# Token halves around the post-norms of the second block, and a weight ring with the low parts written over the raw weights

## The chip, the cores and the metric

One Trainium2 chip, one NeuronCore. The metric is the device time of one launch in microseconds (us). Short names as in the profile: PE is TensorE, DVE VectorE, ACT ScalarE, POOL GpSimd, SP SyncE, which issues the weight DMAs.

## The reference

Two transformer blocks run one after the other on 256 tokens (rows) of width 2048, all in fp32. What matters here is the second block, two layers deep:

```python
for layer in range(DEPTH_2):                          # 2
    h = rms_norm_2(x, mix_pre_g[layer])
    m = mixer_ab(h, ...) if layer % 2 == 0 else mixer_cd(h, ...)   # ends in concat(...) @ w_out
    x = x + rms_norm_2(m, mix_post_g[layer])          # post-norm
    h = rms_norm_2(x, ffn_pre_g[layer])
    f = channel_mixer(h, ...)                         # up, causal conv, gelu(gate) * val, down
    x = x + rms_norm_2(f, ffn_post_g[layer])          # post-norm
```

So there are four post-norms. Each needs the whole row of `m` or `f` (all 2048 columns) before one column of the new `x` is known, and the next projection needs the new `x`, transposed. Three of them are followed by a projection and are called seams here (after `mixer_ab`, after the first `channel_mixer`, after `mixer_cd`); the fourth ends the kernel.

## The kernel before

All weights are read once, as chunks of 256 contraction rows by 512 columns (`CHUNK`, 512 KB; some are narrower), about 1,140 of them. fp32 accuracy is had by splitting every operand in a high and a low part in fp32r: ACT copies a raw chunk to `w_hi` (`split_hi`, L271), DVE subtracts to get `w_lo` (`split_lo`, L277), and PE multiplies each of the two k-tiles of a chunk three times (hi·hi, hi·lo, lo·hi, L302 to L304) for each token half `tt` of 128 rows: 12 matmuls of 512 columns a chunk, in `mm_chunk`. Eight chunks make a block of 512 output columns, accumulated in two PSUM banks (`acc`), one for each token half.

The order of all work is written by hand, engine by engine, with counting semaphores. SP loads chunk after chunk into `raw`, a ring of 8 slots, and issues the load of chunk k when `lo_done` says that chunk k-8 has been split. `w_hi` and `w_lo` are rings of 4 slots (`SPLIT`), so `split_hi` of chunk k also waits until PE has used chunk k-4 (`chunk_used`). DVE and ACT have the splits some four chunks ahead of PE in their programs, with the work on results between them.

```python
wait(sp, lo_done, 8 * q + k - RING + 1)            # load_chunk
wait(act, raw_in[k % RING], 16 * (q + k // RING + 1))   # split_hi
wait(act, chunk_used, 8 * q + k - SPLIT + 1)
```

At a seam the last output block (b = 3) has four chunks in a mixer and eight in an ffn. PE finishes all chunks of it for both token halves, DVE adds the PSUM result to what was kept before (`macc`, L1898 or L1849), ACT squares it (`squares`, L1216, with the sum per row), DVE sums (L1565, L1566), ACT takes the root (L1221, with the load of its function table), DVE the reciprocal (L1570), and `normed` (L1859) adds the scaled row to `xres` for both halves of a 512-column slice. Meanwhile POOL multiplies each slice of `macc` by the gain of the post-norm (`scaled_out`, L850), and `normed` waits for that (`merged`). Then `turn` (L341) transposes a slice of `xres` in 8 matmuls, `turn_hi` (L350) and `turn_lo` (L366) write it as `l_hi` and `l_lo`, and the first projection block runs its chunks with the next `turn` after chunks 1, 3 and 5 (`new_x`, and `turns` in `mm_block`). The gain of the pre-norm goes in with the transposes; the pre-norm's own 1/rms multiplies the projection's output later.

Other places where PE waits for a chain of ACT and DVE are the pooling and index work of `mixer_ab` (L1048, L1063) and the recurrent and attention inputs of `mixer_cd` (L1167, L341, `turned_in`). In both, weights that PE reads straight from `raw` (two chunks each) take slots of the ring; before, they too are split, for nothing. Early in the kernel, POOL loads bias rows for the attention (L814) while narrow chunks (width 268, `A_TAIL`) pass through PE.

Of the kernel before, what the change touches and what calls it, by code (L numbers as in the profile page):

```python
# [16 lines left out]
F32 = mybir.dt.float32  # L17
# [101 lines left out]
def build_program(nc, d):  # L119

    with ExitStack() as ctx:
# [54 lines left out]
        stat_v, stat_a = sem("stat_v"), sem("stat_a")  # L176
        at_t, at_qk, at_s, at_l, at_mx, at_e, at_r, at_p = [sem("at_" + n) for n in ("t", "qk", "s", "l", "mx", "e", "r", "p")]
        at_pt, at_ptc, at_pv, at_pvg, at_ohi, at_o = [sem("at_" + n) for n in ("pt", "ptc", "pv", "pvg", "ohi", "o")]
        out_st, out_ready = sem("out_st"), sem("out_ready")
# [86 lines left out]
        def split_hi(act, q, ks, n=CHUNK):  # L266

            for k in ks:
                wait(act, raw_in[k % RING], 16 * (q + k // RING + 1))
                wait(act, chunk_used, 8 * q + k - SPLIT + 1)  # L270
                nc.scalar.activation(w_hi[:, k % SPLIT, 0:n], raw[:, k % RING, 0:n], ACT.Copy).then_inc(hi_done, 1)  # L271

        def split_lo(dve, q, ks, n=CHUNK):

            for k in ks:
                dve.wait_ge(hi_done, 8 * q + k + 1)
                nc.vector.tensor_tensor(w_lo[:, k % SPLIT, 0:n], raw[:, k % RING, 0:n], w_hi[:, k % SPLIT, 0:n].bitcast(F32),  # L277
                                        ALU.subtract).then_inc(lo_done, 1)

        def a_width(k):  # L280
            b, c = A_ORDER[k] if k < len(A_ORDER) else (0, 0)
            return CHUNK if b is None else 2 * A_BLOCKS[b][1]

        def split_hi_a(act, k0, k1):
            for k in range(k0, k1):
                split_hi(act, 0, (k,), a_width(k))

        def split_lo_a(dve, k0, k1):
            for k in range(k0, k1):
                split_lo(dve, 0, (k,), a_width(k))  # L290

        def mm_chunk(pe, q, k, lhs, kts, out, first, last, w=BW):

            pe.wait_ge(lo_done, 8 * q + k + 1)
            hi = w_hi[:, k % SPLIT, 0:len(kts) * w].rearrange("p (a b) -> p a b", b=w)
            lo = w_lo[:, k % SPLIT, 0:len(kts) * w].rearrange("p (a b) -> p a b", b=w)
# [8 lines left out]
            m.then_inc(chunk_used, 1)  # L305

# [285 lines left out]
        gpost_mix = late[:, 0:D]  # L592

# [35 lines left out]
        T_X1, T_PU, T_ABX, T_F0, T_FX, T_CD, T_CQ, T_QR, T_CDX, T_F1 = 29, 33, 35, 39, 55, 59, 63, 65, 67, 71  # L629
# [15 lines left out]
        HALVES = [t + b for t in (0, T_O, T_X1, T_ABX, T_FX) for b in range(4)] + [T_CQ] + [T_CDX + b for b in range(4)]  # L645
        X_ROWS = {T_ABX: 16, T_FX: 20, T_CDX: 24}
# [21 lines left out]
        A_ORDER += [(5, c) for c in range(NCH)]  # L668
        A_END = [A_ORDER.index((b, NCH - 1)) + 1 for b in range(6)]
# [25 lines left out]
        def _(sp):  # L695
# [85 lines left out]
            for b in range(4):  # L781
                sp.wait_ge(out_ready, b + 1)
                sp.dma_start(d["out"][:, BW * b:BW * (b + 1)].rearrange("(t p) n -> p t n", p=P),
                             xres[:, :, BW * b:BW * (b + 1)]).then_inc(out_st, 16)
# [3 lines left out]
        def _(pool):  # L788
# [54 lines left out]
            def scaled_out(squares0, gwide, gains_in):  # L843

                pool.wait_ge(*gains_in)
                for b in range(4):
# [42 lines left out]
        def _(pe):  # L889
# [11 lines left out]
            def cmp_chunk(n, k):  # L901
# [5 lines left out]
                whi = w_hi[:, k % SPLIT, :].rearrange("p (a b) -> p a b", a=4)  # L907
                wlo = w_lo[:, k % SPLIT, :].rearrange("p (a b) -> p a b", a=4)
# [206 lines left out]
            def mixer_out(q, o, u, other, us, n, e, g):  # L1115
# [8 lines left out]
                out_chunks(q, o, u, OUT_ENDS[0] - 4, OUT_ENDS[3])  # L1124

            def new_x(x_t):

                return lambda b: turn(pe, x_t + b, xres[:, :, BW * b:BW * (b + 1)], (rows_ready, X_ROWS[x_t] + b + 1))

            def ffn(q, o, u, t, x_t, h):  # L1130

                for g in range(2):
                    def pair(j, first=False):
# [3 lines left out]
                        def mine():  # L1137
                            turn(pe, t + 8 * g + 2 * j, hid2, (acc_free, u + 12 * g + 2 * j + 1))
                        mm_block(pe, q + 12 * g + 2 * j, u + 12 * g + 2 * j, 0 if u % 2 == 0 else 1, lh, k0=o,
                                 need=(lhs_ready, x_t) if first and g == 0 else None, hook=None if first else before,  # L1140
                                 turns=new_x(x_t) if first and g == 0 else None)
# [4 lines left out]
                    for b in range(4):  # L1146
                        def last():
                            turn(pe, t + 8 * g + 7, hid2, (acc_free, u + 12 * g + 8))
                        mm_block(pe, q + 12 * g + 8 + b, u + 12 * g + 8 + b, (u + b) % 2, mh, k0=o,
                                 need=(hid_ready, h + 4 * g) if b == 0 else None, hook=last if b == 0 else None)  # L1150

            mixer_out(Q_ABO, O2, U_ABO, (pool_dve, 6), ud, N_D, E_D, G_D)
            ffn(Q_F0, O2, U_F0, T_F0, T_ABX, 0)
# [18 lines left out]
            for b, (c, w) in enumerate(CD_BLOCKS):  # L1172
# [33 lines left out]
            ffn(Q_F1, O6, U_F1, T_F1, T_CDX, 8)  # L1206

        @block.scalar
        def _(act):
            aseq = [0]  # L1210

            def squares(rows, col, sums):
                for tt in range(2):
# [3 lines left out]
                                             accum_out=sums[:, tt, col:col + 1]).then_inc(squares_done, 1)  # L1217

# [186 lines left out]
            def mixer_out(q, o, u, us, n, e, g, k, t, gain):  # L1405
# [3 lines left out]
                for b, end in enumerate(OUT_ENDS):  # L1409
                    split_hi(act, q, range(o + at, o + end + SPLIT))  # L1410
                    at = end + SPLIT
                    act.wait_ge(acc_free, u + 3 + b + 1)
                    squares(macc[:, :, BW * b:BW * (b + 1)], b, ssp)
                new_x(q + 4, o, k, t, gain)

            def new_x(q, o, k, t, gain):

                root(k, ST["root"], ST["mean"])
                for b in range(4):
                    turn_hi(act, t + b, tiles(lh, 4 * b), gain[:, 4 * b:4 * b + 4])  # L1420
                    squares(xres[:, :, BW * b:BW * (b + 1)], b, ssp)
                    if 0 < b < 3:
                        split_hi(act, q, (o + 2 * b + 2, o + 2 * b + 3))
# [687 lines left out]
```

## Time and profile before

| | us |
|---|---|
| runs, median (lowest to highest) | 3404.14 (3403.9 to 3407.31), 3 runs |
| the profiled execution | 3407.14 |
| its span, first to last instruction | 3405.4 |
| PE busy / DVE busy / ACT busy | 3291.9 / 1948.1 / 1664.9 |
| PE not busy in the span | 113.5 |

Mean granted TensorE clock in the span: 0.987. The profiled execution is 1.7 us longer than its span, and 3.0 us above the median of the runs. PE is the engine to watch: an idle microsecond there is a microsecond of the kernel, and idle time of the others counts only where PE waits for it.

### The profile page before, as it was taken

How to read it: one execution, taken by the hardware profiler on the slowest of the kernel's cores; microseconds unless marked ns; L12 is line 12 of the kernel's file. 1: busy time of each engine (PE TensorE's matmuls, PEld its weight loads, DVE VectorE, ACT ScalarE, POOL GpSimd, SP SyncE). 2: the span in 40 equal slices, each digit the busy share in tenths (PEclk: the TensorE clock that was granted, in tenths of full speed). 3: DMA queues.
4: the chain of work that ended last, by engine and by line, in shares of the span. 5: the costliest groups of instructions: out<-in, count | busy, mean ns of one | idle time of the engine just before them, and what ended most of it. 6: DMA issues, size and time to landing. Idle time of an engine off the chain costs nothing.

```text
span 3405.4 us, 41414 instructions
## 1 busy us (share of the span) xinstructions
PE 3291.9 (97%) x15346; PEld 2737.7 (80%) x15346; DVE 1948.1 (57%) x2331; ACT 1664.9 (49%) x2256; POOL 184.7 (5%) x199
## 2 busy tenths in 40 slices
PE   8999999999999999999999899999989798999998
PEld 7888778888888888888877788888878677888886
DVE  5566545555555555556555666556655656664665
ACT  5555544444444444445444455445545645553553
POOL 0023100000000000001001100000000011000001
PEclk9999999999999999999999999999989899999999
DMA  8845556666666666655565556566554544656653
GB/s 258 235 140 154 165 177 193 189 185 193 187 190 191 188 184 190 192 175 172 153 192 159 183 162 185 190 187 184 185 159 127 169 138 161 184 188 195 184 180 131
DMA packets 324437, 608.82 MB, mean 179 GB/s; under 512 B 19468, under 2 KB 46424, under 8 KB 323632
## 3 DMA queue, kind: packets, MB, share of 16 engines
q1 hardware_dynamic: 320768, 594.05, 56.7%
q0 software_dynamic: 3504, 12.52, 1.3%
q8 instruction: 109, 1.79, 0.2%
q14 instruction: 56, 0.46, 0.0%
HBM read 603.22 MB, written 3.28 MB: 178 GB/s over the span
## 4 chain that ended last, share of the span: by engine, by line
PE 94%; DVE 2%; ACT 1%; issue 1%; DMA 0%; POOL 0%; SPq 0%; DVEq 0%; ACTq 0%
PE ps L302 29%; PE ps L304 29%; PE ps L303 29%; PE ps L341 2%; PE ps L444 1%; PE ps L468 1%; ACT w_hi L271 1%; DVE w_lo L277 0%; PE ps L433 0%; POOL main L834 0%; PE ps L470 0%; DVE xres L1859 0%; DVE stats L1566 0%; PE ps L446 0%; PE ps L914 0%
## 5 line engine op out<-in xcount | busy, mean ns | idle before, releaser
L277 DVE TENSOR_TENSOR w_lo<-raw,w_hi 128x1024 fp32r<-128x1024 f32 (+1 forms) x1142 | 1420.7, 1252 | 1244.3 <-ACT w_hi L271 1239.3
L271 ACT ACTIVATE w_hi<-raw 128x1024 fp32r<-128x1024 f32 (+1 forms) x1142 | 1197.0, 1054 | 1509.3 <-PE ps L304 1472.8
L302 PE MATMUL ps<-w_hi,l_hi 128*128 128x512 f32 (+2 forms) x2848 | 1113.4, 391 | 14.0 <-issue 6.4
L303 PE MATMUL ps<-w_lo,l_hi 128*128 128x512 f32 (+2 forms) x2848 | 1098.9, 386 | 1.5 <-issue 1.5
L304 PE MATMUL ps<-w_hi,l_lo 128*128 128x512 f32 (+2 forms) x2848 | 1099.3, 386 | 0.0
L302 PEld LDWEIGHTS ps<-w_hi,l_hi 128*128 128x128 f32 x2848 | 538.0, 189 | 121.7 <-issue 10.8
L302 PE MATMUL ps<-w_hi,m_hi 128*128 128x512 f32 (+1 forms) x1600 | 624.0, 390 | 10.4 <-DVE main L1883 5.5
L304 PEld LDWEIGHTS ps<-w_hi,l_lo 128*128 128x128 f32 x2848 | 537.7, 189 | 107.0
L303 PEld LDWEIGHTS ps<-w_lo,l_hi 128*128 128x128 f32 x2848 | 538.5, 189 | 102.1 <-issue 1.9
L304 PE MATMUL ps<-w_hi,m_lo 128*128 128x512 f32 (+1 forms) x1600 | 620.0, 387 | 0.0
L303 PE MATMUL ps<-w_lo,m_hi 128*128 128x512 f32 (+1 forms) x1600 | 619.9, 387 | 0.0
L302 PEld LDWEIGHTS ps<-w_hi,m_hi 128*128 128x128 f32 x1600 | 302.2, 189 | 71.4 <-DVE main L1883 6.2
L304 PEld LDWEIGHTS ps<-w_hi,m_lo 128*128 128x128 f32 x1600 | 302.1, 189 | 61.3
L303 PEld LDWEIGHTS ps<-w_lo,m_hi 128*128 128x128 f32 x1600 | 302.3, 189 | 59.5
L1914 DVE SCALAR_TENSOR_TENSOR main<-ps,main 128x255 f32<-128x255 f32 (+1 forms) x256 | 105.8, 475 | 19.9 <-ACT main L1449 18.8
L1227 ACT ACTIVATE main<-ps,stats 128x512 f32<-128x512 f32 (+2 forms) x170 | 104.9, 667 | 9.5 <-PE ps L304 9.4
L341 PE MATMUL ps<-ident_sb,main 128*128 128x128 f32 x494 | 65.6, 276 | 13.9 <-DVE main L2035 4.3
L850 POOL TENSOR_TENSOR main<-main 128x1024 f32<-128x1024 f32 x8 | 19.1, 2386 | 1088.0 <-ACT ps L1216 1088.0
L341 PEld LDWEIGHTS ps<-ident_sb,main 128*128 128x128 f32 x494 | 57.9, 142 | 23.7 <-DVE main L2035 4.7
L341 PE MATMUL ps<-ident_sb,xres 128*128 128x128 f32 x192 | 30.0, 308 | 41.3 <-DVE xres L1859 27.9
L366 DVE SCALAR_TENSOR_TENSOR l_lo<-ps,pk_sb,l_hi 128x256 fp32r<-128x256 f32 x96 | 39.8, 476 | 47.3 <-ACT l_hi L350 47.3
L350 ACT ACTIVATE l_hi<-ps,pk_sb 128x256 fp32r<-128x256 f32 x96 | 37.6, 473 | 55.7 <-PE ps L341 55.6
(293 smaller groups left out, 1544.0 us busy)
## 6 DMA issues: line engine op xcount, KB each, us to landing
raw<-ffn_up SPq DMA_DIRECT2D x256, 512.0 KB, 4.1
raw<-w_in SPq DMA_DIRECT2D x176, 512.0 KB, 3.7
raw<-w_mlp_in SPq DMA_DIRECT2D x128, 512.0 KB, 3.8
raw<-w_mlp_out SPq DMA_DIRECT2D x128, 512.0 KB, 3.9
raw<-ffn_down SPq DMA_DIRECT2D x128, 512.0 KB, 4.6
raw<-ab_w_in SPq DMA_DIRECT2D x64, 512.0 KB, 3.8
raw<-w_branch SPq DMA_DIRECT2D x48, 512.0 KB, 3.9
raw<-cd_w_in SPq DMA_DIRECT2D x40, 512.0 KB, 4.3
```

The costliest lines, as they stand in the source:

```text
L271: nc.scalar.activation(w_hi[:, k % SPLIT, 0:n], raw[:, k % RING, 0:n], ACT.Copy).then_inc(hi_done, 1)
L277: nc.vector.tensor_tensor(w_lo[:, k % SPLIT, 0:n], raw[:, k % RING, 0:n], w_hi[:, k % SPLIT, 0:n].bitcast(F32), ALU.subtract).then_inc(lo_ ...
L302: nc.tensor.matmul(o, xh, hi[:, j, :], start=first and j == 0, stop=False)
L303: nc.tensor.matmul(o, xh, lo[:, j, :], start=False, stop=False)
L304: m = nc.tensor.matmul(o, xl, hi[:, j, :], start=False, stop=last and j == len(kts) - 1)
L341: m = nc.tensor.transpose(tp4[:, j, tt * P:(tt + 1) * P], rows[:, tt, j * P:(j + 1) * P], ident[:])
L350: i = nc.scalar.activation(dst[0][:, j, :], tp4[:, j, :], ACT.Copy, scale=gain[:, j:j + 1])
L366: i = nc.vector.scalar_tensor_tensor(dst[1][:, j, :], tp4[:, j, :], gain[:, j:j + 1], dst[0][:, j, :].bitcast(F32), ALU.mult, ALU.subtract)
L444: m = nc.tensor.matmul(o, qs[:, tt * P:(tt + 1) * P], kt[:, 0:w], start=True, stop=u.rope is None)
L468: m = nc.tensor.matmul(o, u.v[0][0:kk, :], pts[0:kk, 0:TOK], start=u.first, stop=u.last and len(u.v) == 1)
L1227: i = nc.scalar.activation(dst(tt), acc(par, w)[:, tt, :], func, scale=scale[:, tt:tt + 1])
L1914: i = nc.vector.scalar_tensor_tensor(dst[:, x, n:], tp4[:, x, 0:TOK - n], fcw[:, 2 - n, k:k + 1], dst[:, x, n:], ALU.mult, ALU.add)
```

## The change

Three parts.

1. **The seams by token halves.** The last four chunks before a post-norm are multiplied first for token half 0 (`last_chunks`, first loop), then for half 1. While PE does half 1, DVE, ACT and DVE carry half 0 through the add (`last_half`), the square and root (`post_root`), the reciprocal and `normed`, now on 128 rows by 512 columns each. PE's turns are of 4 transposes (`turn_half`), each into PSUM banks of its own pair (`x_bank`, banks 4 to 7 in turn). The next block's first four chunks are again multiplied by halves (`first_block`). The gain product of slice 3 goes from POOL to DVE. The function table for the root is loaded early (`sqrt_table`). The squares are written to SBUF (`junk`) instead of PSUM. The fourth post-norm, at the end, goes by halves as well, and the output is stored by halves.
2. **The ring.** `w_lo` lies over `raw` (8 slots, written in place), and `w_hi` has 8 slots. So `split_hi` waits for its load alone, and the load of chunk k waits until PE has used chunk k-8.
3. **Widths.** Chunks that are narrower than 512 columns are split at their own width throughout (`WIDTH`: the three `AB_TAIL` blocks of 368 columns, the last of `mixer_cd`'s, of 320), and the four chunks that PE reads raw are not split at all.

The diff below is cut to the ring, PE's two new functions, the first half of ACT's `seam`, and SP's stores at the end.

```diff
-        raw = sb("raw", [P, RING, CHUNK])
-        w_hi = sb("w_hi", [P, SPLIT, CHUNK], F32R)
-        w_lo = sb("w_lo", [P, SPLIT, CHUNK], F32R)
+        raw_guard = nc.sbuf_tensor("raw", [P, RING, CHUNK], F32)
+        raw = raw_guard.__enter__()
+        raw_guard.__exit__(None, None, None)
+        w_lo = sb("w_lo", [P, RING, CHUNK], F32R)
+        w_hi = sb("w_hi", [P, RING, CHUNK], F32R)
...
-            wait(sp, lo_done, 8 * q + k - RING + 1)
+            wait(sp, chunk_used, 8 * q + k - RING + 1)
...
-                wait(act, chunk_used, 8 * q + k - SPLIT + 1)
...
+            def last_chunks(s, q, k, kt0, out, first):
+                for i in range(4):
+                    kt = kt0 + 2 * i
+                    m = mm_half(pe, q, k + i, mh, (kt, kt + 1), out, 0, first and i == 0, i == 3)
+                m.then_inc(tt_done, 1)
+                for i in range(4):
+                    kt = kt0 + 2 * i
+                    m = mm_half(pe, q, k + i, mh, (kt, kt + 1), out, 1, first and i == 0, i == 3)
+                    m.then_inc(chunk_used, 1)
+                    if s < 3 and i > 1:
+                        turn_half(s, i - 2)
+            def first_block(s, q, k, out):
+                def turned(c, tt):
+                    pe.wait_ge(xt_lo, 16 * s + 2 * X_TURNS.index((c // 2, tt)) + c % 2 + 1)
+                for c in range(4):
+                    turned(c, 0)
+                    mm_half(pe, q, k + c, lh, (2 * c, 2 * c + 1), out, 0, c == 0, False)
+                    if c > 1:
+                        turn_half(s, c)
+                for c in range(4):
+                    turned(c, 1)
+                    m = mm_half(pe, q, k + c, lh, (2 * c, 2 * c + 1), out, 1, c == 0, False)
+                    m.then_inc(chunk_used, 1)
+                    turn_half(s, 4 + c)
+                for c in range(4, NCH):
+                    turned(c, 1)
+                    mm_chunk(pe, q, k + c, lh, (2 * c, 2 * c + 1), out, False, c == NCH - 1)
...
+            def seam(s, q, o, k0, gain):
+                sqrt_table()
+                split_hi(act, q, range(o + k0, o + 4))
+                post_root(s, 0)
+                x_square(s, 0)
+                x_square(s, 1)
+                x_hi(s, 0, gain)
+                x_hi(s, 1, gain)
+                post_root(s, 1)
+                split_hi(act, q, (o + 4, o + 5))
...
+            for tt in range(2):
+                for h in range(2):
+                    sp.wait_ge(x_rows, 24 + 4 * tt + 2 * h + 2)
+                    sp.dma_start(d["out"][P * tt:P * (tt + 1), 2 * BW * h:2 * BW * (h + 1)],
+                                 xres[:, tt, 2 * BW * h:2 * BW * (h + 1)]).then_inc(out_st, 16)
```

DVE's part of a seam is `split_lo` of the chunks up to o+3, the sums of slices 0 to 2, `last_half` of half 0, `post_rstd`, `normed` of slices 0 and 1, `x_lo` of turn 0, then `last_half` of half 1, and so on. What each engine's program holds there:

ACT, at the first seam (after `mixer_ab`), before. The first two rows are the splits of the next projection's chunks 2 and 3; L1216 squares slice 3 of `macc`.

```order
L271 ACTIVATE w_hi<-raw 128x1024 [waits chunk_used,raw_in4]
L271 ACTIVATE w_hi<-raw 128x1024 [waits chunk_used,raw_in5]
L1216 ACTIVATE ps,stats<-main 128x512 [waits squares_done,acc_free]
L1216 ACTIVATE ps,stats<-main 128x512 [waits squares_done]
L1221 ACT_TABLE_LOAD
L1221 ACTIVATE stats<-stats 128x2 [waits stat_v]
L350 ACTIVATE l_hi<-ps,pk_sb 128x256 [waits tp_done]
L350 ACTIVATE l_hi<-ps,pk_sb 128x256 x3
```

The same place now. The first two rows square slice 2, whose result comes at the start of the last four chunks.

```order
L1320 ACTIVATE late,stats<-main 128x512 [waits squares_done,acc_free]
L1320 ACTIVATE late,stats<-main 128x512 [waits squares_done]
L1534 ACT_TABLE_LOAD
L1534 ACTIVATE stats<-ident_sb 128x1
L284 ACTIVATE w_hi<-raw 128x1024 [waits raw_in3]
L284 ACTIVATE w_hi<-raw 128x1024 [waits raw_in4]
L284 ACTIVATE w_hi<-raw 128x1024 [waits raw_in5]
L1320 ACTIVATE late,stats<-main 128x512 [waits squares_done,half_out]
L1530 ACTIVATE stats<-stats 128x1 [waits squares_done,post_v]
L1320 ACTIVATE late,stats<-xres 128x512 [waits squares_done,x_rows] x2
L1546 ACTIVATE l_hi<-ps,pk_sb 128x128 [waits xt_pe]
```

The splits wait for their load alone, and three of them and the table load now stand between the squares of slice 2 and the square of half 0 of slice 3.

DVE, at the same seam, before:

```order
L277 TENSOR_TENSOR w_lo<-raw,w_hi 128x1024 [waits hi_done] x4
L1898 TENSOR_TENSOR main<-ps,main 128x2x512 [waits acc_free,chunk_used]
L1565 TENSOR_REDUCE stats<-stats 128x2 [waits squares_done]
L1566 TENSOR_SCALAR stats<-stats 128x2 [waits dve_seq]
L1570 RECIPROCAL stats<-stats 128x2 [waits stat_a]
L1859 SCALAR_TENSOR_TENSOR xres<-main,stats,xres 128x512 [waits merged,stat_v]
```

and now:

```order
L2115 TENSOR_TENSOR main<-ps,main 128x2x512 [waits acc_free,chunk_used]
L295 TENSOR_TENSOR w_lo<-raw,w_hi 128x1024 [waits hi_done] x3
L2012 TENSOR_REDUCE stats<-stats 128x2 [waits squares_done]
L2013 TENSOR_SCALAR stats<-stats 128x2 [waits dve_seq]
L2023 TENSOR_TENSOR main<-ps,main 128x512 [waits gain_in,acc_free,tt_done]
L2026 TENSOR_TENSOR main<-main,late 128x512 [waits half_out]
L2034 RECIPROCAL stats<-stats 128x1 [waits post_a,dve_seq]
L2042 SCALAR_TENSOR_TENSOR xres<-main,stats,xres 128x512 [waits merged,dve_seq]
```

The add of slice 3 has become two, of which the first waits for half 0 alone (`tt_done`), behind three splits; the gain product (L2026) is new on DVE.

## Rows read from the trace of the kernel before

**Rows 1.** The page, busy time and share of the span

```profile
PE 3291.9 (97%) x15346; PEld 2737.7 (80%) x15346; DVE 1948.1 (57%) x2331; ACT 1664.9 (49%) x2256; POOL 184.7 (5%) x199
```

**Rows 2.** Who PE waited for: total us, times, longest

```profile
PE ps L341 <- DVE xres L1859: 27.9, 3, 9.3
PE ps L1063 <- issue: 6.7, 1, 6.7
...
PE ps L302 <- DVE m_lo L366: 4.4, 1, 4.4
...
PE ps L341 <- ACT main L1227: 3.7, 1, 3.7
```

**Rows 3.** Timeline of the first seam: start, us, engine, what, idle before

```profile
1947.57 0.39 PE L304 MATMUL ps<-w_hi,m_lo 128*128 128x512 f32 x1
1948.05 1.06 ACT L271 ACTIVATE w_hi<-raw 128x1024 fp32r<-128x1024 f32 x1 [1.66 <-PE ps L304]
1950.28 1.22 DVE L1898 TENSOR_TENSOR main<-ps,main 128x1024 f32<-128x1024 f32 x1
...
1955.78 2.74 DVE L1859 SCALAR_TENSOR_TENSOR xres<-main,stats,xres 128x512 f32<-128x512 f32 x4
1957.25 1.97 PE L341 MATMUL ps<-ident_sb,xres 128*128 128x128 f32 x8 [9.29 <-DVE xres L1859]
1961.10 0.77 PE L302 MATMUL ps<-w_hi,l_hi 128*128 128x512 f32 x1 [1.89 <-issue]
1966.30 1.04 PE L341 MATMUL ps<-ident_sb,xres 128*128 128x128 f32 x8
1972.66 1.04 PE L341 MATMUL ps<-ident_sb,xres 128*128 128x128 f32 x8
```

**Rows 4.** Window there: us, busy of PE PEld DVE ACT POOL, clock, DMA, GB/s

```profile
1961.10:1966.30 5.20, 5.20 (x13) 3.99 (x13) 2.00 (x4) 0.94 (x4) 0.00 (x0) 0.51 0.00 0
```

**Rows 5.** Groups by shape: count, busy us, mean ns of one

```profile
L350 ACT ACTIVATE l_hi<-ps,pk_sb 128x256 fp32r<-128x256 f32 x96 | 37.6, 473 | 55.7 <-PE ps L341 55.6
L1216 ACT ACTIVATE ps<-main 128x512 f32<-128x512 f32 x34 | 20.1, 592 | 47.4 <-DVE main L1849 28.0 <-DVE main L1898 14.6 <-DVE main L1896 4.8
L487 ACT ACTIVATE main<-main,stats 128x128 f32<-128x128 f32 x32 | 12.5, 389 | 0.0
```

**Rows 6.** Timeline and clock after two waits of PE in `mixer_cd`

```profile
2619.26 1.99 PE L1167 MATMUL ps<-main,raw 128*128 128x256 f32 x8 [2.69 <-ACT main L1475]
2644.70 0.50 PE L302 MATMUL ps<-w_hi,l_hi 128*128 128x512 f32 x1 [2.68 <-DVE w_lo L277]
...
2619.00:2624.00 5.00, 4.74 (x21) 4.02 (x22) 1.23 (x1) 2.72 (x6) 0.00 (x0) 1.00 0.31 85
2644.70:2649.00 4.30, 4.30 (x12) 3.39 (x13) 2.21 (x2) 4.27 (x8) 0.00 (x0) 0.60 0.84 253
```

**Rows 7.** Timeline of the end

```profile
3390.68 0.39 PE L304 MATMUL ps<-w_hi,m_lo 128*128 128x512 f32 x1
3396.60 5.39 DVE L1859 SCALAR_TENSOR_TENSOR xres<-main,stats,xres 128x512 f32<-128x512 f32 x8
```

**Rows 8.** Weight loads while bias rows are loaded, 100 to 220 us

```profile
157.72 1.06 ACT L271 ACTIVATE w_hi<-raw 128x1024 fp32r<-128x1024 f32 x1 [4.52 <-DMA raw<-w_in]
...
DMA to landing us min/median/max: 2.7/4.0/16.0
```

**Rows 9.** A narrow split, and two splits of the pooling stage

```profile
118.53 0.65 ACT L271 ACTIVATE w_hi<-raw 128x536 fp32r<-128x536 f32 x1 [0.35 <-PE ps L914]
1707.83 1.06 ACT L271 ACTIVATE w_hi<-raw 128x1024 fp32r<-128x1024 f32 x1 [0.38 <-PE ps L304]
1713.27 1.06 ACT L271 ACTIVATE w_hi<-raw 128x1024 fp32r<-128x1024 f32 x1 [1.66 <-PE ps L304]
```

**Rows 10.** Timeline of ACT in `mixer_cd`: a table load and what follows it

```profile
2636.03 1.28 ACT L1475 ACT_TABLE_LOAD   x1
2637.32 1.57 ACT L1475 ACTIVATE main<-ps,pk_sb 128x256 f32<-128x256 f32 x4
```

More of the change, by code:

```diff
@@ L280, in a_width @@
[L280 to L290, printed above, removed]
+                if n == 0:
+                    dve.wait_ge(lo_done, 8 * q + k)
+                    dve.sem_inc(lo_done, 1)
+                    continue
@@ L592, in build_program @@
         gpost_mix = late[:, 0:D]
+        junk = [late[:, 2944 + BW * j:2944 + BW * (j + 1)] for j in range(2)]
         zc = view(main, 0, 2, CD_X)
@@ L845, in scaled_out @@
                 pool.wait_ge(*gains_in)
-                for b in range(4):
+                for b in range(3):
                     pool.wait_ge(squares_done, squares0 + 2 * b + 2)
@@ L1217, in squares, with square, squares_m @@
                                              accum_out=sums[:, tt, col:col + 1]).then_inc(squares_done, 1)
+            def square(row, total):
+                wait(act, squares_done, aseq[0] - 1)
+                aseq[0] += 1
+                nc.scalar.activation(junk[aseq[0] % 2], row, ACT.Square, scale=float(D) ** -0.5,
+                                     accum_out=total).then_inc(squares_done, 1)
+            def squares_m(b):
+                for tt in range(2):
+                    square(macc[:, tt, BW * b:BW * (b + 1)], ssp[:, tt, b:b + 1])
             def root(k, out, mean):
@@ L1414, in mixer_out @@
[L1414 to L1423, printed above, removed]
-                root(k + 1, ST["root"], ST["mean"])
-                act.wait_ge(stat_v, 2 * k + 4)
@@ L1427, in ffn, with post_root @@
-            def ffn(q, o, u, t, c0, layer, end):
+                    squares_m(b)
+            def post_root(s, tt):
+                act.wait_ge(half_out, 2 * s + tt + 1)
+                square(macc[:, tt, 3 * BW:4 * BW], ssp[:, tt, 3:4])
+                if tt == 0:
+                    act.wait_ge(post_v, s + 1)
+                act.wait_ge(squares_done, aseq[0])
+                nc.scalar.activation(ST["root2"][:, tt:tt + 1], ssp[:, tt, 3:4], ACT.Sqrt, bias=ST["tmp0"][:, tt:tt + 1]).then_inc(post_a, 1)
@@ new lines, in seam @@
+            def seam(s, q, o, k0, gain):
[8 more added lines that the diff above has]
+                split_hi(act, q, (o + 4, o + 5))
+                for i in (2, 3, 4):
+                    x_hi(s, i, gain)
+                split_hi(act, q, (o + 6,))
+                for i in (5, 6, 7):
+                    x_hi(s, i, gain)
+                split_hi(act, q, (o + 7,))
+                for i in range(2, 8):
+                    x_square(s, i)
+                act.wait_ge(next_v, s + 1)
+                nc.scalar.activation(ST["root"], ST["tmp2"], ACT.Sqrt).then_inc(next_a, 1)
@@ L1428, in ffn @@
+            def ffn(s, q, o, u, t, c0, layer):
                 act.wait_ge(gain_in, 16 * (4 + 4 * layer))
```

327 lines of the change are left out of this document (227 added, 100 removed).

## The prediction

> **What bounds the kernel now.** The page comes first: PE is busy for 3291.9 us, 97% of the span, and no other engine passes 57% [rows 1]. So only PE's idle time and PE's time at a low clock can be won. The list of waits says where it idles. The largest entry is the transposes of `xres` behind `normed`: 27.9 us in three waits of 9.3, one a seam. The next are a 6.7 us wait in `mixer_ab`'s index stage and waits of 4.4 and 3.7 in `mixer_cd` [rows 2].
>
> The timeline of the first seam shows what the 9.3 hides. The last matmul ends at 1947.96. ACT then makes one more split, because that split had waited for this very chunk; only then comes the add at 1950.28, `normed` at 1955.78, and the transposes at 1957.25. These take 1.97 where later turns take 1.04, then PE waits another 1.89 for the low parts, and the twelve matmuls of the first chunk run until 1966.30 [rows 3] at a granted clock of 0.51, which is the 1.2 GHz level of the two [rows 4]. A chunk at full clock takes 2.72: two splits that each waited for PE stand 5.44 apart over two chunks [rows 9]. Two chunks and a turn take 6.36 [rows 3], so a turn costs 0.92. From 1947.96 to 1966.30 are 18.34 us with 2.72 + 0.92 = 3.64 of work in them: **14.7 us lost a seam, 44.1 in three** (the others show the same 9.3).
>
> At the end the last matmul is over at 3391.07 and the span at 3405.4: 14.3 us. The last `normed` ends at 3401.99, so the stores take the last 3.4 [rows 7].
>
> **The seams, step by step.** I set T = 0 where PE starts half 0 of the last four chunks. Half a chunk is 1.36, so half 0 ends at 5.4, and turn 0 is due after three half chunks of half 1, at 9.5. At seams 1 and 3 (after the mixers) DVE's and ACT's programs have this ahead of it:
> - the add of slice 2, 1.22 [rows 3], ends at 1.3;
> - two squares of 592 ns, each with a read of its sum (about 0.15, estimate), end at 2.8 [rows 5];
> - table load and a first root, 1.28 + 0.2 [rows 10], to 4.3;
> - three splits on ACT at 1.0, to 7.3, the last of them on DVE to 8.7;
> - sums of two tiny operations, 0.35; add of half 0, half of 1.22 and some fixed part, 0.66; to 9.8;
> - square 0.75, root 0.2, reciprocal 0.2, one `normed` at 2.74 / 4 = 0.69: turn 0 can start at 11.8.
>
> So PE waits 2.3 at turn 0. A second wait, 0.5, comes before the first half chunk of the projection: ACT squares two new slices before it turns to `x_hi`. After that PE takes 1.36 + 0.46 = 1.82 for a half chunk with a half turn, and DVE needs four `x_lo` and a `normed` in it. No row shows a copy of 128x128 out of PSUM. Spaced ACT copies of 128x256 start 0.39 apart against a mean of 473 ns each, and a 128x128 activation within SBUF takes 389 ns [rows 5], which by the same overlap is 0.3 apart; below is 0.2 (half of 0.39), above 0.39 (no cheaper than 256 columns). I take 0.3, nearest to the shown shape: DVE then needs 1.2 + 0.69 = 1.89 and is late by under 0.1 a step, 0.5 in all. At 0.39 it is late by 0.4 a step and a seam costs 2.5 more; at 0.2 nothing.
>
> Waits at seams 1 and 3 are then 3.3 each. The clock: after one wait of 2.69 it stayed at 1.00, after one of 2.68 it stood at 0.60 for the next 4.3 us [rows 6], which loses 0.4 x 4.3 = 1.7. I charge 1.2 for a wait of 2.3 (bounds 0 and 1.7): **4.5 a seam**.
>
> The Trainium skill ("ScalarE: Activation LUTs", What ACT_TABLE_LOAD costs) puts a change of table at about 1.28 us plus a drain of about 1.38. The drain would stand ahead of the three splits and move turn 0 by 1.4 at seams 1 and 3, and the forecast to 3361. The trace disagrees: the activation behind a table load starts 0.01 us after it [rows 10].
>
> Seam 2 (after the ffn) has its last block of eight chunks, so slice 2 is done eleven microseconds before T = 0. Only the split of the projection's chunk 3 presses: its load leaves when PE has used the chunk eight before it, at T = 0, lands at 4.0 (the median) [rows 8], is split by 6.2, and `normed` ends at 9.1, before turn 0 is due. **0.6.**
>
> The transposes are as many as before. POOL's product of slice 3 went (2.3 us beside DVE's work) and costs DVE 0.66, off the path since it runs beside ACT's square. The squares' other target costs nothing that a row shows. The pre-norm's six late squares hold ACT some 4.5 us, with the next block's chunks not due for 5 more; if that cover is gone, they cost what is missing of it. Seams: 44.1 - 4.5 - 4.5 - 0.6 = **34.5 won**.
>
> **The end.** After PE's last matmul only half 1 is left: 0.66 + 0.75 + 0.2 + 0.2, four `normed` of 0.69, hops of 0.2, and 3.4 for the stores: 8.1 in place of 14.3. **6.2 won.**
>
> **The ring and the widths.** (a) Where ACT had to wait for PE before a split, and PE then waited for what stands behind that split, the wait goes. In the index stage ACT's splits waited for PE up to 1713.27 [rows 9], and DVE's work for the 6.7 us wait stands behind the last. Freed, it comes 2.7 earlier; a like place in the pooling stage gives 1. I take 3.5 (bounds 0 and 6.7). (b) In `mixer_cd` the waits of 3.7 and 4.4 end an ACT chain. Seven of its splits are now 640 columns wide: 1.06 less 0.65 for 488 columns fewer [rows 9] gives 0.32 each, 2.3; freed splits add 1.2 and 1.4. I take 5 (bounds 0 and 8). (c) Against it: a load now leaves 8 chunks before PE needs it, where it was nearly 12 (four in the split ring, eight raw). In steady state that is 21.8 us for a landing of 4.0, hidden. But where bias rows are loaded, a weight load took 16.0 us to land, and ACT stood 4.5 us for one at 157.72, with nothing of it reaching PE [rows 8]. The chunks before it are narrow (1.46 us each at PE, estimate from 268 columns against 512), so eight of them lead by under 12. I charge 3 (bounds 0 and 8). Sum **5.5**.
>
> **The sum.** 34.5 + 6.2 + 5.5 = 46.2 off the profiled execution's 3407.1 is 3360.9. That execution stands 3.0 above the median of the runs, so I forecast **3358**.
>
> **Rivals.**
> 1. *As worked out*, 3358, own range 3350 to 3367. Chance 0.64.
> 2. *ACT and DVE become the bound inside the seam*: 0.39 for each 128x128 operation, and a clock that falls at all three. A seam then costs some 9.5, 15.6 are won of 44.1: 3404 - 15.6 - 6.2 - 5.5 = 3377. For it: DVE has 1.89 to do in 1.82. Against it: each step has slack on ACT. 0.14.
> 3. *The ring gives more*: no clock loss, no late load, (a) and (b) near their upper bounds: 3404 - 37.5 - 6.2 - 12 = 3348. For it: ACT's splits waited for PE all over the kernel. Against it: few of PE's waits stand behind such a split. 0.13.
> 4. *Half 0 is not carried beside half 1*, because DVE and ACT come to it only after the splits whose loads wait for PE. Only end and ring pay: 3392. It would need those loads 9 us late. 0.04.
> 5. *Slower: loads too late in steady state.* Each of 1,140 chunks has its load leave only when PE is eight chunks away. If PE lost 0.04 us a chunk (46.2 / 1,140), 1.5% of 2.72, nothing would be left; at 0.06, 3426. It decides when landings pass 21.8 less 2.3 for the splits, 19.5 us; the median is 4.0 and the longest seen 16.0. 0.03, and 0.02 for landing within 0.2% of before.
>
> The range reaches to rival 2 and most of rival 3: 3345 to 3377. A difference of 0.2% (6.8 us) is about what a measurement of this kernel tells from none. Rivals 1 to 4 are faster: 0.95; same 0.02; slower 0.03.
>
> **What would show it.** In the trace after: no 9.3 us wait; at seams 1 and 3 one wait of 2 to 3 us before the first half turn (turn 0), behind `normed`; at seam 2 none over 1; 8 us from last matmul to end. The 6.7 us wait in the index stage near 4, the pair in `mixer_cd` at 5 together. Around 160 us PE idle for 2 to 4, behind `w_lo`, ACT behind a DMA. The forecast is wrong if `x_lo` steps leave PE waiting at every half turn, if the clock stays low through a seam, or if ACT waits for loads in the ffn blocks.

## The result, and the profile after

The changed kernel takes 3344.18 us (median of 4, 3343.87 to 3345.6) against 3404.89 of the kernel before (4 runs, 3403.9 to 3407.31): a ratio of 0.9821, 95% interval 0.9804 to 0.9838. The direction and most of the parts were as forecast, the size was not: 46.2 us were to come off the profiled execution, and its span fell by 61.6, from 3405.4 to 3343.8. The result lies 0.8 below the low end of the range.

The page's first row, as in [rows 1], shows PE busy for 10.7 us less and idle for 50.9 less. The matmuls are the same in number; the mean granted clock went from 0.987 to 0.995:

```profile
PE 3281.2 (98%) x15346; PEld 2730.0 (82%) x15346; DVE 1899.6 (57%) x2391; ACT 1621.4 (48%) x2308; POOL 187.4 (6%) x195
```

Who PE waited for, as in [rows 2] (total us, times, longest):

```profile
PE ps L1103 <- issue: 4.7, 1, 4.7
PE ps L1175 <- DVE xres L2042: 4.5, 2, 2.3
...
PE ps L309 <- DVE m_lo L391: 2.9, 1, 2.9
...
PE ps L366 <- ACT main L1335: 1.0, 1, 1.0
```

The three waits of 9.3 at the seams are two of 2.26; the 6.7 of the index stage is 4.7; the 4.4 and 3.7 of `mixer_cd` are 2.9 and 1.0.

PE runs 15,346 matmuls in both kernels. The start of the n-th one before, less its start after, is what has been won up to there. Read at the stages' borders (in the seams, where the order differs, from border to border) this gives a ledger of the whole 61.6. The third column is the same for another profiled execution of the changed kernel, from a later run:

| place (start before, us) | won | won, second profile | forecast |
|---|---|---|---|
| to 165, narrow chunks beside the bias rows | -2.9 | -3.4 | -3 |
| 671 to 775, four transposes behind a POOL add | 3.3 | 3.3 | 0 |
| 1218 to 1222, a block's end | 2.2 | 1.0 | 0 |
| 1585, a block's end | 2.2 | 2.3 | 0 |
| 1695 and 1720, pooling and index | 2.6 | 3.1 | 3.5 |
| 1839, transposes ahead of `mixer_ab`'s last projection | 2.6 | 2.5 | 0 |
| seam 1 | 10.7 | 11.9 | 10.2 |
| seam 2 | 15.0 | 15.2 | 14.1 |
| `mixer_cd`, 2600 to 2725 | 7.7 | 7.6 | 5 |
| seam 3 | 11.7 | 11.6 | 10.2 |
| the end | 6.5 | 6.5 | 6.2 |

So an entry can move by up to 1.2 from one execution to the next; the sum is the same.

The timeline of seam 1 after (beside [rows 3]), on ACT, DVE, POOL and PE in order of start:

```profile
1927.11 1.22 DVE L2115 TENSOR_TENSOR main<-ps,main 128x1024 f32<-128x1024 f32 x1 [0.16 <-PE ps L311]
...
1929.72 1.28 ACT L1534 ACT_TABLE_LOAD   x1
1929.78 2.40 POOL L890 TENSOR_TENSOR main<-main,late 128x1024 f32<-128x1024 f32 x1 [8.46 <-ACT late L1320]
...
1931.13 2.94 ACT L284 ACTIVATE w_hi<-raw 128x1024 fp32r<-128x1024 f32 x3
1932.20 3.50 DVE L295 TENSOR_TENSOR w_lo<-raw,w_hi 128x1024 fp32r<-128x1024 f32 x3 [3.87 <-ACT w_hi L284]
...
1935.91 0.69 DVE L2023 TENSOR_TENSOR main<-ps,main 128x512 f32<-128x512 f32 x1
1936.64 0.63 ACT L1320 ACTIVATE late<-main 128x512 f32<-128x512 f32 x1 [2.56 <-DVE main L2023]
...
1937.85 0.16 DVE L2034 RECIPROCAL stats<-stats 128x1 f32<-128x1 f32 x1 [0.52 <-ACT stats L1530]
1938.04 1.41 DVE L2042 SCALAR_TENSOR_TENSOR xres<-main,stats,xres 128x512 f32<-128x512 f32 x2
1938.85 1.04 PE L1175 MATMUL ps<-ident_sb,xres 128*128 128x128 f32 x4 [2.26 <-DVE xres L2042]
...
1940.76 1.13 DVE L2051 SCALAR_TENSOR_TENSOR l_lo<-ps,pk_sb,l_hi 128x128 fp32r<-128x128 f32 x4 [1.31 <-ACT l_hi L1546]
```

The wait is 2.26 where 2.3 was forecast, behind `normed`, as the ledger of the seam had it: three splits from 1931.13 to 1935.7, and only then the add of half 0. Four 128x128 `x_lo` take 1.13, so 0.28 each, where I had taken 0.3. Granted clock behind the same wait of 2.26 at seam 1 and at seam 3 (columns as in [rows 4]):

```profile
1938.85:1942.25 3.40, 3.40 (x10) 2.71 (x11) 1.73 (x5) 2.39 (x8) 0.00 (x0) 0.52 0.43 163
2793.45:2796.85 3.40, 3.30 (x18) 2.62 (x19) 2.09 (x6) 3.28 (x12) 0.00 (x0) 1.00 0.56 190
```

So one of two fell to the lower level. At 0.52 for 3.40 us that is at most 1.6 us of loss; I had charged 1.2 for each. In the second profile the waits are 2.26 and 2.27, and the clock stood at 1.00 behind both; at seam 1:

```profile
1940.11:1943.51 3.40, 3.31 (x18) 2.64 (x19) 2.10 (x6) 3.27 (x12) 0.00 (x0) 1.00 0.46 161
```

There seam 1 won 1.2 more, which is what the lower level cost by the two ledgers. The end, as in [rows 7]: the last matmul ends at 3335.99, the last `normed` at 3340.8, the span at 3343.8. That is 7.8 us; 8.1 was forecast.

```profile
3335.60 0.39 PE L329 MATMUL ps<-w_hi,m_lo 128*128 128x512 f32 x1
...
3338.04 2.74 DVE L2042 SCALAR_TENSOR_TENSOR xres<-main,stats,xres 128x512 f32<-128x512 f32 x4
```

Of the 15.4 us that were missed, 10.3 lie at four places for which the sum had no term, 2.7 in `mixer_cd`, 2.9 in the seams and 0.3 at the end, less 0.9 in the index stage. The rest is rounding. The timeline of the block's end at 1585 shows a mechanism that could do it. Before:

```profile
1577.64 0.39 PE L304 MATMUL ps<-w_hi,m_lo 128*128 128x512 f32 x1
1578.12 1.06 ACT L271 ACTIVATE w_hi<-raw 128x1024 fp32r<-128x1024 f32 x1 [1.66 <-PE ps L304]
1579.22 1.23 DVE L277 TENSOR_TENSOR w_lo<-raw,w_hi 128x1024 fp32r<-128x1024 f32 x1 [1.49 <-ACT w_hi L271]
1580.36 1.22 DVE L1693 TENSOR_TENSOR xres<-ps,xres 128x1024 f32<-128x1024 f32 x1
...
1583.02 2.34 POOL L842 TENSOR_TENSOR xres<-xres,late 128x1024 f32<-128x1024 f32 x1 [20.27 <-ACT ps L1216]
1585.42 1.09 PE L341 MATMUL ps<-ident_sb,xres 128*128 128x128 f32 x8 [3.37 <-POOL xres L842]
```

and after:

```profile
1575.05 0.39 PE L311 MATMUL ps<-w_hi,m_lo 128*128 128x512 f32 x1
...
1575.47 1.23 DVE L1849 TENSOR_TENSOR xres<-ps,xres 128x1024 f32<-128x1024 f32 x1 [1.47 <-PE ps L311]
...
1578.15 2.38 POOL L882 TENSOR_TENSOR xres<-xres,late 128x1024 f32<-128x1024 f32 x1 [20.31 <-ACT ps L1313]
1580.58 1.09 PE L366 MATMUL ps<-ident_sb,xres 128*128 128x128 f32 x8 [1.12 <-POOL xres L882]
```

Before, the block's last matmul ends at 1578.03 and the add of its result starts at 1580.36, 2.33 later: on DVE it stands behind the low part of a split which had waited on ACT for that same matmul. After, the add starts 0.03 behind PE, and the wait at the transposes is 2.25 shorter. That is my theory: **every operation that stood behind a split in ACT's or DVE's program came up to 2.3 us after the end of the block it was for, and the change frees it**, at block ends all over the kernel and in the seams too. The rivals are the widths, and the other timing of the loads.

### The profile page after: what moved, and what is told of

It is laid out like the page before. It is cut to its first block, busy times and chain, and to the rows that moved or that the text cites. A ratio compares the mean times of both kernels' runs of the same rounds, so it can differ in the third digit from the quotient of the medians.

```text
span 3343.8 us, 40463 instructions
## 1 busy us (share of the span) xinstructions
PE 3281.2 (98%) x15346; PEld 2730.0 (82%) x15346; DVE 1899.6 (57%) x2391; ACT 1621.4 (48%) x2308; POOL 187.4 (6%) x195
## 4 chain that ended last, share of the span: by engine, by line
PE 95%; DVE 2%; ACT 1%; DMA 1%; issue 0%; POOL 0%; SPq 0%; DVEq 0%; ACTq 0%
PE ps L309 29%; PE ps L311 29%; PE ps L310 29%; PE ps L366 2%; PE ps L469 1%; DVE w_lo L295 1%; PE ps L493 1%; DMA raw<-w_in 1%; PE ps L327 1%; PE ps L329 1%; PE ps L328 1%; PE ps L458 0%; ACT w_hi L284 0%; PE ps L1175 0%; PE ps L495 0%
## 5 line engine op out<-in xcount | busy, mean ns | idle before, releaser
L295 DVE TENSOR_TENSOR w_lo<-raw,w_hi 128x1024 fp32r<-128x1024 f32 (+3 forms) x1138 | 1366.2, 1238 | 783.1 <-ACT w_hi L284 779.5
L284 ACT ACTIVATE w_hi<-raw 128x1024 fp32r<-128x1024 f32 (+3 forms) x1138 | 1143.2, 1044 | 656.6 <-DMA raw<-w_mlp_out 130.3
L309 PE MATMUL ps<-w_hi,l_hi 128*128 128x512 f32 (+3 forms) x2800 | 1091.5, 390 | 9.7 <-DVE w_lo L295 5.1
L311 PE MATMUL ps<-w_hi,l_lo 128*128 128x512 f32 (+3 forms) x2800 | 1078.5, 385 | 0.0
L310 PE MATMUL ps<-w_lo,l_hi 128*128 128x512 f32 (+3 forms) x2800 | 1077.8, 385 | 0.0
L309 PE MATMUL ps<-w_hi,m_hi 128*128 128x512 f32 (+1 forms) x1536 | 598.3, 389 | 8.9 <-DVE main L2099 5.5
L310 PE MATMUL ps<-w_lo,m_hi 128*128 128x512 f32 (+1 forms) x1536 | 594.2, 387 | 0.0
L311 PE MATMUL ps<-w_hi,m_lo 128*128 128x512 f32 (+1 forms) x1536 | 594.2, 387 | 0.0
L1599 ACT ACTIVATE main<-ps,main 128x256 f32<-128x256 f32 x128 | 61.9, 564 | 80.7 <-PE ps L366 80.7
L1849 DVE TENSOR_TENSOR xres<-ps,xres 128x1024 f32<-128x1024 f32 x20 | 24.5, 1225 | 78.1 <-PE ps L311 78.1
```

The costliest lines, as they stand in the source:

```text
L284: nc.scalar.activation(w_hi[:, k % RING, 0:n], raw[:, k % RING, 0:n], ACT.Copy).then_inc(hi_done, 1)
L295: nc.vector.tensor_tensor(w_lo[:, k % RING, 0:n], raw[:, k % RING, 0:n], w_hi[:, k % RING, 0:n].bitcast(F32), ALU.subtract).then_inc(lo_do ...
L309: nc.tensor.matmul(o, xh, hi[:, j, :], start=first and j == 0, stop=False)
L310: nc.tensor.matmul(o, xh, lo[:, j, :], start=False, stop=False)
L311: m = nc.tensor.matmul(o, xl, hi[:, j, :], start=False, stop=last and j == len(kts) - 1)
L1599: i = nc.scalar.activation(dst[:, x, :], tp4[:, x, :], ACT.Identity, scale=fcw[:, 2, k:k + 1], bias=fcb[:, k:k + 1])
```

## The experiments

### The widths alone

The kernel before, with part 3 alone:

```diff
+                n = width(q, k, n)
                 nc.scalar.activation(w_hi[:, k % SPLIT, 0:n], raw[:, k % RING, 0:n], ACT.Copy)
```

> The kernel before with the third part alone: narrow chunks split at their own width (368 and 320 columns), the four raw chunks not split. Theory A (what the change won outside the seams and the end, 17.7 us by the two traces, came from splits that no longer wait for PE): the widths are worth 2 to 3, so 3401 to 3402. Theory B (the widths gave most of it): 3390 to 3395. The prediction priced the widths at 2.3.

Measured: 3401.62 against 3404.15, ratio 0.9992 (0.9983 to 1.0001); span 3402.2, so 3.2 less in the profile. That is where theory A had it, but the interval holds 1, so the whole is at the edge of what can be told from nothing; theory B's 3390 to 3395 falls. The matmul ledger puts 0.3 of it in `mixer_cd` and 1.6 in seam 2, where the clock stayed low for less time (13.7 us in place of 17.1). The 0.3 hides more than it shows. PE's waits of 3.7 and 4.4 became 2.9 and 3.9, so the widths took 1.3 off them, and behind the wait of 2.7 at 2617 the clock fell where before it had not, which cost 1.6; a later low stretch was 3.4 us shorter.

### The ring with and without its freed splits

Parts 2 and 3 on the kernel before; the first of the two keeps the wait of `split_hi`.

```diff
-            wait(sp, lo_done, 8 * q + k - RING + 1)
+            wait(sp, chunk_used, 8 * q + k - RING + 1)
...
                 wait(act, chunk_used, 8 * q + k - SPLIT + 1)   # kept in the first, gone in the second
```

> The kernel before with the new ring (low part over raw, eight slots, a load leaves when PE has used the chunk eight before it) and the widths, but each ACT split still waits until PE has used the chunk four before it. So only the load's later start is added to the widths. Theory A: the starved stretch at 140 to 165 us comes in and costs 3, the waits of the other places stay: 3404 to 3405. Theory B (the new load timing is what helps): below 3398. A third reading, that the later loads are the cost I feared at more places: above 3410.

> As the one with the held splits, without that wait: parts 2 and 3 of the change whole, no seam by halves. Theory A: the 17.7 of the ledger, and at each of the three seams the add of the last slice comes 2.3 sooner, since no split stands before it that waited for the last chunk: 3404 - 17.7 - 6.9 = 3379. As the prediction sized the ring and widths (5.5): 3398. Theory B, ring and widths help only together with the seams: 3395 or more.

With the wait: 3405.72, ratio 1.0004 (0.9995 to 1.0013), span 3403.1. Without it: 3385.31, ratio 0.9945 (0.9931 to 0.9958), span 3378.9. One wait of ACT is 20.4 us in the medians and 24.2 in the spans. Theory A had forecast 3379 for the second; the median is 6 above that, with five executions from 3379.95 to 3391.08, and the profiled one near their low end. The block's end at 1585 in the kernel without it reads as in the changed one:

```profile
1575.77 1.22 DVE L1712 TENSOR_TENSOR xres<-ps,xres 128x1024 f32<-128x1024 f32 x1 [1.41 <-PE ps L319]
...
1580.87 1.09 PE L356 MATMUL ps<-ident_sb,xres 128*128 128x128 f32 x8 [1.11 <-POOL xres L861]
```

and with it as before:

```profile
1581.67 1.22 DVE L1713 TENSOR_TENSOR xres<-ps,xres 128x1024 f32<-128x1024 f32 x1
...
1586.73 1.10 PE L357 MATMUL ps<-ident_sb,xres 128*128 128x128 f32 x8 [2.83 <-POOL xres L862]
```

The waits of 0.63 before the four transposes behind POOL are there with the wait (four times) and not without it. Place by place the freed splits give, by the ledgers of the two kernels, 3.4 at these, 3.3 at 1585, 3.1 in pooling and index, 1.0 at 1839, 5.0 in `mixer_cd` and 7.6 in the three seams. These hold the clock of each execution too: at 1585 the waits differ by 1.7, and the other 1.6 is a clock that fell there with the held splits and did not fall before.

Two parts of the changed kernel's gain are not theirs. The 2.2 at 1220 came with the wait kept too (2.0), and not with the widths alone; PE's two waits there, 0.74 and 1.46 before, are put down to nothing that the profile shows. It is 1.0 to 2.2 in the profiles of the kernels with the new ring, so its cause stays open. And of the 2.6 at 1839 the wait is only 1.0: PE waited 2.41 in the kernel with the held splits as before, and yet 1.6 was won behind it, since there the clock did not fall.

At the seams, still by whole chunks, PE's wait at the turn goes from three of 9.3 to

```profile
PE ps L356 <- DVE xres L1878: 21.0, 3, 7.0
```

which is the 2.3 each of the expectation. The ledger of this kernel gives 17.1 outside seams and end, the changed one 17.7. The rival of the loads falls but for the 2.0 at 1220: with the wait kept, the new load timing costs 3.7 before 165 us, and the whole is no faster than before.

### The wait put back in the changed kernel

```diff
+                if not (isinstance(q, int) and 8 * q + k in AT_SEAM):
+                    wait(act, chunk_used, 8 * q + k - SPLIT + 1)
```

> The changed kernel with one wait put back: an ACT split waits until PE has used the chunk four before it, except for the eight chunks behind each seam. Theory A (freed splits let the adds and scalings behind them start when PE's block ends): the places outside seams and end lose again what they won, about 17 by the pair of runs with and without this wait: 3344 + 17 = 3361. Rival (the seams by halves had freed them as well, so the wait costs little here): 3344 to 3350.

Measured: 3376.87, ratio to before 0.9915 (0.9901 to 0.9928), span 3375.1, 31.3 more than the changed kernel. Both sizes expected, 17 and at most 6, were too small. Outside the seams the places lose what they had won, 19.0 in all with the lower clock behind some of them. The other 12.3 is in the seams, though their own eight chunks were exempt:

```profile
1939.58 2.01 ACT L286 ACTIVATE w_hi<-raw 128x1024 fp32r<-128x1024 f32 x2 [1.66 <-PE ps L313]
1940.67 2.36 DVE L297 TENSOR_TENSOR w_lo<-raw,w_hi 128x1024 fp32r<-128x1024 f32 x2 [1.31 <-ACT w_hi L286]
1942.95 1.22 DVE L2118 TENSOR_TENSOR main<-ps,main 128x1024 f32<-128x1024 f32 x1
...
1954.69 1.11 PE L1178 MATMUL ps<-ident_sb,xres 128*128 128x128 f32 x4 [5.69 <-DVE xres L2045]
```

The last chunk of the block waits for the one four before it, slice 2 is added 3.4 late, and the wait at turn 0 is 5.69 in place of 2.26. So about half of what the change brings hangs on the freed splits, part of it inside the seams. No run has the seams by halves on the old ring; this one is the nearest to it.

### The splits moved at the seams

Chunk 1 of the next projection is split ahead of the last four chunks, chunk 2 ahead of the table load, chunk 3 behind it and, on DVE, behind the add of half 0. In the second kernel DVE's split of chunk 2 also goes behind that add, and that of chunk 3 behind the first two `normed`; on ACT the first `x_hi` goes ahead of the square of the second new slice. The diff shows ACT's part of the first kernel.

```diff
-                    to = end + SPLIT + b // 2
+                    to = end + SPLIT + (0, 0, 2)[b]
...
+                split_hi(act, q, range(o + k0, o + 3))
                 sqrt_table()
-                split_hi(act, q, range(o + k0, o + 4))
+                split_hi(act, q, (o + 3,))
```

> The changed kernel with the splits of the next projection's chunks moved at seams 1 and 3: chunk 1 ahead of the last four chunks, chunk 2 ahead of the table load, chunk 3 behind it on ACT, and on DVE behind the add of half 0. Theory A (the three splits between slice 2's squares and the add of half 0 set the 2.26 us wait): both waits go, 4.5, and the 3.4 us at half clock behind the first of them, 1.7: 3338. Rival (the table load and the squares set it, or DVE then is late at a later half turn): 3342 to 3345, with a new wait at a later turn.

> The kernel with early splits, and on DVE the split of chunk 2 behind the add and product of half 0, that of chunk 3 behind the first two normed; ACT's squares of the new slices one before and one behind the first copies. Theory A (DVE's splits ahead of the reciprocal are all that is late; one took 2.57 us beside POOL's product, where it takes 1.23 alone): turn 0 on time at seams 1 and 3, 1.4 each off the kernel with early splits: 3340. Rival (what is moved behind turn 0 makes a later half turn or the first half chunk wait): 3342 to 3345, with a wait of 0.7 or more inside the seam.

> The changed kernel once more, beside the next two on one chip: 3344.

> The kernel with the splits moved twice once more. Its profile lay 5.3 below that of the changed kernel; if that is the edit and not the start of the execution, the medians stand 3 to 5 apart, 3339 to 3341. If they stand under 1 apart, the gain at the two seams is given back elsewhere.

The first gave 3343.01 (0.9821, 0.9807 to 0.9834; span 3340.9): both waits went from 2.26 to 1.4, not to nothing as theory A had it, and the new wait at a later turn that the rival named did not come. Why shows on DVE and POOL in it:

```profile
1930.33 2.40 POOL L890 TENSOR_TENSOR main<-main,late 128x1024 f32<-128x1024 f32 x1 [9.35 <-ACT late L1320]
1931.24 2.57 DVE L295 TENSOR_TENSOR w_lo<-raw,w_hi 128x1024 fp32r<-128x1024 f32 x1 [2.36 <-ACT w_hi L284]
```

The DVE split is over 1.1 us after POOL's product instead of 1.23 us after its own start, so the add of half 0 behind it comes 1.3 later than with a split of 1.23: about the whole of the 1.4. No run takes POOL's product away from there; the next kernel takes the split away. It gave 3340.31 (0.9813, 0.98 to 0.9827; span 3338.5), with no wait over 0.6 left in any seam. Beside each other on one chip the changed kernel took 3345.13 (span 3343.8) and this one 3340.62 (span 3339.5): 4.5 in the medians, 4.3 in the spans, which the matmul ledger puts at seam 1 (2.5) and seam 3 (2.0). It is the fastest kernel here. The two intervals against before overlap (0.981 to 0.9837, 0.9799 to 0.9825), but run side by side, all five executions of the one (3339.7 to 3341.57) lie below all five of the other (3343.68 to 3345.57), and the ledger says where.

### The function table loaded late

```diff
                 split_hi(act, q, range(o + k0, o + 3))
-                sqrt_table()
                 split_hi(act, q, (o + 3,))
```

> As the one with the splits moved twice, without the early load of the root's function table: it is loaded where the root is due. By the rows (1.28 for the load, 0.01 to the activation behind it) the root comes 1.28 later, the reciprocal 0.9 later, since DVE's split holds it until then, and each of three seams loses up to 0.9: 3340.3 + 2.7 = 3343. Rival, a load that is followed by a drain of 1.38 as the Trainium skill (ScalarE: Activation LUTs, What ACT_TABLE_LOAD costs) has it: 2.3 at each seam, 3347.

Measured 3343.08 (0.9817, 0.9804 to 0.983; span 3341.3), 2.5 over its neighbour in the medians and 1.8 in the spans; the two sets of five executions overlap. Seam 1 in it:

```profile
1935.44 1.28 ACT L1530 ACT_TABLE_LOAD   x1
1936.73 0.30 ACT L1530 ACTIVATE stats<-stats 128x1 f32<-128x1 f32 x1
...
1938.07 0.66 PE L1175 MATMUL ps<-ident_sb,xres 128*128 128x128 f32 x4 [0.56 <-DVE xres L2042]
```

The activation starts 0.01 behind the load, also where nothing but the root waits for it. A drain of 1.38 between them, which the Trainium skill (ScalarE: Activation LUTs, What ACT_TABLE_LOAD costs) adds to each change of table, is not in this trace. With it each seam was to lose 2.3; PE's longest wait in a seam is 0.56.

That the medians stand 2.5 apart, close to the 2.7 expected, is in part luck. By the ledger the three seams lose 0.6, 0.4 and 0.1, and not up to 0.9 each. Another 1.1 is in `mixer_cd`, at a wait of 4.03 in place of 2.91 at the same instruction, which the edit does not touch; the clock had fallen at other places in the two executions.

### The bias rows stored in thirds

The changed kernel with the store in three parts. The places that the second and third part read have been written anew by then, so the attention bias of those heads is another one.

```diff
-            pool.dma_start(scr, r_rows.unsqueeze(1).to_broadcast([24, BIAS_ROWS, 384])).then_inc(scr_st, 16)
...
+                pool.dma_start(scr[h0:h0 + HEADS], r_rows[h0:h0 + HEADS]. ...).then_inc(scr_st, 16)
```

> The changed kernel with the 1152 KB store of the bias rows in three parts, each just ahead of the loads that read it. Theory A (the store, issued 0.3 us ahead of a weight load, made that load land after 11.4 us, and PE lost 3 between 141 and 164 us): PE's waits there shrink to under 1, 3341 to 3342. Rival (the loads of the bias rows, 140.7 to 145, do it): the waits stay, 3344.

> Both edits together: the bias rows stored in thirds and the splits moved twice. If they add, 3344 - 4.3 - 2.7 = 3337; if either falls, as the other alone.

Measured 3355.57 (0.9854, 0.9839 to 0.9869) and 3348.25 (0.9832, 0.9819 to 0.9846), spans 3348.6 and 3350.4: both slower, and theory A, that the size of the store makes the loss, falls. The profiled execution of the first is 5.2 faster than its median, so its trace shows only a part of what the kernel loses. In the changed kernel the rows around 140 us are

```profile
129.38 0.85 POOL L846 DMA_DIRECT2D bias_rows<-late  x1 [120.64 <-DVE late L1731]
...
141.08 3.61 ACT L284 ACTIVATE w_hi<-raw 128x536 fp32r<-128x536 f32 x5 [7.56 <-DMA raw<-w_in]
142.53 0.39 PE L309 MATMUL ps<-w_hi,l_hi 128*128 128x268 f32 x1 [1.33 <-DVE w_lo L295]
```

The store of 1152 KB took 11.0 us to land there. A third of it took

```profile
bias_rows<-late POOLq DMA_DIRECT2D x1, 384.0 KB, 10.0
```

nearly as long. Between 127 and 165 us PE lost 2.4 in the first kernel, against 2.8 in the changed one, but 5.4 in the second with the same stores, against 2.9 and 4.3 in its neighbours; so nothing was won there. The third part pushed the loads of its bias rows to 349 us, beside loads of `w_branch`, whose median landing there went from 3.8 to

```profile
raw<-w_branch SPq DMA_DIRECT2D x4, 512.0 KB, 12.0
...
366.23 2.13 ACT L284 ACTIVATE w_hi<-raw 128x1024 fp32r<-128x1024 f32 x2 [5.30 <-DMA raw<-w_branch]
367.28 0.79 PE L309 MATMUL ps<-w_hi,l_hi 128*128 128x512 f32 x1 [7.06 <-DVE w_lo L295]
```

So the loss stands where POOL's small transfers and a short lead meet, but which of the store and the eight loads of bias rows makes it at 141 us stays open. That the new load timing is its cause is shown: 2.4 to 5.4 are lost there in the kernels with the new ring, and nothing with the widths alone.

## Why the prediction was right in direction and short in size

- **What bounds it**: right. PE's idle time and low clock were the whole of the 61.6.
- **The seams**: 34.5 forecast with the end apart, 37.4 measured. Turn 0 was forecast at T + 11.8 and came at T + 11.9, with T at 1926.91, PE's first matmul of half 0; the wait of 2.3 was 2.26. The second wait of 0.5 at the projection and the steps that should be late by under 0.1 left no wait over 0.6. The clock fell behind one of two waits, and behind none of two in the second profile: 1.2 and nothing where 2.4 was charged. At seam 2 the clock had stayed low longer before than at the others (0.93 in the 6.36 us in which they show 1.00), and nothing was lost at turn 0. My 14.7 held what a late add had put in it, the split at 1948.05 in [rows 3]; I priced that it went, without asking where else it stood.
- **The end**: 6.2 forecast, 6.5 measured.
- **(c), the late loads**: 3 forecast, 2.9 measured, behind an ACT that waited 7.56 for a load.
- **(a), the freed splits, is the step that failed.** "Where ACT had to wait for PE before a split, and PE then waited for what stands behind that split, the wait goes" is what the runs show. I then priced it at the two stages whose waits stood high in the list, 3.5 with an upper bound of 6.7. It measures 2.6 there, and 6.5 at places whose single waits, 0.63 to 3.37, I had given no term (four transposes, 1585, 1839). Two more gains, 2.2 at 1220 and 1.6 at 1839, came for the other reasons above. The row that shows how often a split waited was in the waits of ACT before, and I had not read it for its count (it does not give PE's loss):

```profile
ACT w_hi L271 <- PE ps L304: 1472.8, 966, 4.5
```

966 of the 1,142 splits stood behind PE; after, no such row is left. I should have gone through every wait of PE in the kernel and asked whether a split stood ahead of its releaser. For `mixer_cd`, (b), it is the same: 5 forecast, 7.7 measured. The pair of waits that I priced gave 4.2: the widths 1.3 and not 2.3, the freed splits 2.9 where 2.6 was forecast. What has no term is two more waits that the freed splits shortened, of 2.7 at 2619 by 1.0 and of 4.3 at 2707 by 1.6; the last 1 or so is clock.
- **Rival 3** ("the ring gives more", 3348) is the case that came nearest, with a loss by late loads that it had left out and, in one of two profiles, a fall of the clock. Its reason against, that few of PE's waits stand behind such a split, was the error. Rivals 2 and 4 did not come. Rival 2's price of 9.5 a seam is 2.0 more than its own terms give (4.5, and 2.5 for the copies, and 0.5 for the clock), so the upper end of my range stood higher than I had grounds for; this did not matter here. Rival 5 had its mechanism, at one place.

## What to carry to other kernels

A producer is here the engine that fills a buffer (ACT, with its splits), a consumer the one that reads it (PE). A producer that waits in order for a consumer's buffer is not only late itself: it holds every short operation queued behind it, and these may be what the consumer waits for next. Count the waits of such an instruction over the whole kernel and look behind each, small waits too, before pricing a deeper ring. Where work moves onto a path beside another engine's operation (DVE beside POOL here), check that the two run together in the trace.

## What the runs showed of the hardware

DVE and POOL do not always run together. While POOL multiplied for 2.40 us, a DVE operation on two columns took 2.28 us; the same one in the changed kernel took 0.17. From the kernel with the splits moved twice:

```profile
1931.66 0.16 DVE L2013 TENSOR_REDUCE stats<-stats 128x2 f32<-128x6 f32 x1 [1.40 <-ACT late L1320]
1931.70 2.41 POOL L890 TENSOR_TENSOR main<-main,late 128x1024 f32<-128x1024 f32 x1 [9.37 <-ACT late L1320]
1931.85 2.28 DVE L2014 TENSOR_SCALAR stats<-stats 128x2 f32<-128x2 f32 x1
1934.04 0.68 DVE L2024 TENSOR_TENSOR main<-ps,main 128x512 f32<-128x512 f32 x1
```

The reduction that started before POOL was not held; the next operation ended with POOL. The Trainium skill (SBUF — State Buffer, Who interferes with whom) has this rule: the two engines share one pair of ports under an exclusive lock, and the one that comes second is blocked for the whole instruction. The trace agrees, with 2.28 for 0.17 and, for a split, 2.57 for 1.23. I had not weighed it: in my seam POOL's product of slice 2 ran free beside DVE. In the changed kernel it ended at 1932.18, when DVE's first split was due at 1932.20, and cost nothing.

The same wait of PE does not always bring the lower clock. Behind the four waits of 2.26 and 2.27 us in the two profiles of the changed kernel, the granted clock was 0.52 over the next 3.40 us once and 1.00 three times, with 1.2 us between the two executions at that seam. A difference of that size between two traces has to be looked up in the clock before it is put down to an edit.
